# Latent attention: low halves of seven outputs and most of the paired q rotation move from VectorE to GpSimd, and the rotated q is copied four places later

## The reference, cut to what matters

```
q = (rms_norm(c_q) @ w_qup)            # 8 heads x (128 nope + 64 rope)
q_pe = rotate(q_rope)                  # t1*cos - t2*sin , t2*cos + t1*sin
s = (q_nope . k_nope + q_pe . k_pe) * scale
p = softmax(s)                         # 512 x 768 per head
o = p @ v ;  y = (o * silu(gate)) @ w_out
```

## Time and profile before

| | us |
|---|---|
| median of three timed runs | 1469.66 |
| the profiled execution's own time | 1466.62 |
| its span, first to last instruction | 1464.8 |
| PE busy | 1388.1 (95%) |
| DVE busy | 742.8 (51%) |
| ACT busy | 576.0 (39%) |
| POOL busy | 500.7 (34%) |
| attention stage, from the first scores (156.35) to the last output tile (320.04) | about 164 |

### The profile page before, as it was taken

One profiled execution on the slowest core, in us unless ns is written; L12 is line 12 of the kernel. 1 busy time (PEld: TensorE's weight loads), 2 busy tenths in 40 slices (PEclk: granted clock), 3 DMA queues, 4 the chain that ended last, 5 costly groups with the idle time before them and its releaser, 6 DMA issues.

```text
span 1464.8 us, 17904 instructions
## 1 busy us (share of the span) xinstructions
PE 1388.1 (95%) x6739; PEld 1137.9 (78%) x6739; DVE 742.8 (51%) x1003; ACT 576.0 (39%) x873; POOL 500.7 (34%) x231
## 2 busy tenths in 40 slices
PE   5899899998799999999999999989999999999998
PEld 2388677776588888877779879878888888888887
DVE  2399688841925536667543542561645435253342
ACT  4243455542433354455543343353244223132231
POOL 1134001136242295411133213214465444444441
PEclk9999999999899999999999879989999999999999
DMA  9685000117231243311223213213333333333332
GB/s 317 190 282 186 20 11 25 30 44 235 70 88 43 58 133 96 87 44 58 61 58 87 58 29 86 57 29 111 90 99 89 100 101 100 88 98 100 98 90 72
DMA packets 204500, 136.15 MB, mean 93 GB/s; under 512 B 7034, under 2 KB 185835, under 8 KB 204443
## 3 DMA queue, kind: packets, MB, share of 16 engines
q1 hardware_dynamic: 204442, 135.37, 30.8%
HBM read 130.64 MB, written 4.72 MB: 92 GB/s over the span
## 4 chain that ended last, share of the span: by engine, by line
PE 79%; DVE 11%; ACT 3%; DMA 2%; issue 2%; SPq 2%; POOL 1%; ACTq 0%; DVEq 0%; POOLq 0%
PE psum L1806 26%; PE psum L1807 24%; PE psum L1808 24%; DVE neg_max L1375 1%; DMA w_raw<-in_mla_w_in 1%; DVE pt_lo L1368 1%; PE psum L1847 1%; DVE probs L1363 1%; DMA w_raw<-in_fno_w_in 1%; POOL w_lo L596 1%; ACT probs L812 1%; PE psum L2172 1%; ACT w_hi L695 1%; PE psum L2298 0%; DVE stage L1721 0%
## 5 line engine op out<-in xcount | busy, mean ns | idle before, releaser
L596 POOL TENSOR_TENSOR w_lo<-w_raw,w_hi 128x1024 fp32r<-128x1024 f32 x180 | 437.9, 2436 | 789.8 <-ACT w_hi L695 661.8
L1806 PE MATMUL psum<-u_hi,w_hi 128*128 128x512 f32 x896 | 362.3, 404 | 14.4 <-DVE u_lo L1463 8.5
L1807 PE MATMUL psum<-u_lo,w_hi 128*128 128x512 f32 x896 | 352.7, 394 | 0.0
L1808 PE MATMUL psum<-u_hi,w_lo 128*128 128x512 f32 x896 | 352.2, 393 | 0.0
L695 ACT ACTIVATE w_hi<-w_raw 128x1024 fp32r<-128x1024 f32 x180 | 189.3, 1055 | 207.2 <-PE psum L1808 155.7
L1806 PEld LDWEIGHTS psum<-u_hi,w_hi 128*128 128x128 f32 x896 | 170.8, 191 | 60.2 <-issue 17.0
L1808 PEld LDWEIGHTS psum<-u_hi,w_lo 128*128 128x128 f32 x896 | 170.6, 190 | 36.7
L1807 PEld LDWEIGHTS psum<-u_lo,w_hi 128*128 128x128 f32 x896 | 171.0, 191 | 35.0 <-issue 1.9
L1806 PE MATMUL psum<-y_hi,w_hi 128*128 128x512 f32 x416 | 162.4, 390 | 0.0
L1807 PE MATMUL psum<-y_lo,w_hi 128*128 128x512 f32 x416 | 161.9, 389 | 0.0
L1808 PE MATMUL psum<-y_hi,w_lo 128*128 128x512 f32 x416 | 161.8, 389 | 0.0
(11 more groups left out here) (406 smaller groups left out, 2325.7 us busy)
## 6 DMA issues: line engine op xcount, KB each, us to landing
w_raw<-in_w_in SPq DMA_DIRECT2D x52, 512.0 KB, 3.7
w_raw<-in_w_up SPq DMA_DIRECT2D x32, 512.0 KB, 4.0
w_raw<-in_w_down SPq DMA_DIRECT2D x32, 512.0 KB, 3.9
ada_back<-in_w_ada SPq DMA_DIRECT2D x7, 2048.0 KB, 8.2
ada_w<-in_w_ada SPq DMA_DIRECT2D x5, 2048.0 KB, 9.3
w_raw<-in_fno_w_in SPq DMA_DIRECT2D x16, 512.0 KB, 3.8
w_raw<-in_mla_w_in SPq DMA_DIRECT2D x11, 512.0 KB, 8.8
w_raw<-in_mla_w_out SPq DMA_DIRECT2D x8, 512.0 KB, 3.9
```

The lines of the kernel that those rows point to most:

```text
L596: pool.tensor_tensor(WL[:, j, :], RAW[:, j % 2, :], f(WH[:, j, :]), ALU.subtract).then_inc(lo_done, 1)
L1806: pe.matmul(out, ah, bh, start=first, stop=False)
L1807: pe.matmul(out, ah, bl, start=False, stop=False)
L1808: return pe.matmul(out, al, bh, start=False, stop=last)
```

## The change

POOL takes over three of the four instructions of the rotation of q for heads 2, 4 and 6 (with their partners), while the shuffle stays on DVE. POOL also takes over the low halves of outputs 0 to 6; the one of the last head stays on DVE. For odd j the high and the low copy of ROPED (ACT and DVE) move from the first place of the next head's units to the place behind K_CTX. Even j keep their place. DVE's `output(j)` gets a wait for POOL's low half of output j-1, because both use the same half of `stage`. The two loads of cos and sin now count on the semaphore of the t5 loads, so that DVE's first use of the t5 tile waits for them too, and the old wait is gone.

```diff
-        s_rope = sem("rope_loaded")
+        un_swap = sem("unit_rope_swapped")
...
-        units = [(0, u) for u in first_units + (TURNED,)]
+        products = [(0, u) for u in first_units + (TURNED,)]
+        units = list(products)
         for j in range(HEADS):
-            units += [(j + 1, ROPED)] * (j < LAST) + [(j - 1, O_LAT)] * (j > 0) + [(j + 1, u) for u in (NOPED, K_LAT, K_CTX)] * (j < LAST)
+            roped, rest = [(j + 1, ROPED)] * (j < LAST), [(j - 1, O_LAT)] * (j > 0) + [(j + 1, u) for u in (NOPED, K_LAT, K_CTX)] * (j < LAST)
+            products += roped + rest
+            units += rest + roped if j % 2 else roped + rest
...
-            sp.dma_start(COS[:], d["rope_cos"]).then_inc(s_rope, 16)
-            sp.dma_start(SIN[:], d["rope_sin"]).then_inc(s_rope, 16)
+            sp.dma_start(COS[:], d["rope_cos"]).then_inc(s_t5, 16)
+            sp.dma_start(SIN[:], d["rope_sin"]).then_inc(s_t5, 16)
...
-            for h in range(HEADS):
+            def rope(j):
+
+                pool.wait_ge(un_raw, j // 2)
+                pool.wait_ge(un_lo, unit_no(j - 1, ROPED))
+                pool.tensor_tensor(QPF[:], QPR[:], COS[:], ALU.mult).then_inc(un_e, 1)
+                pool.wait_ge(un_swap, j // 2)
+                pool.tensor_tensor(SQ[:, 0, :], SQ[:, 0, :], SIN[:], ALU.mult).then_inc(un_e, 1)
+                pool.wait_ge(un_e, 3 * (j // 2))
+                pool.tensor_tensor(QPF[:], QPF[:], SQ[:, 0, :], ALU.add).then_inc(un_e, 1)
+
+            def output_lo(j):
+                pool.wait_ge(o_hi, j + 1)
+                pool.tensor_tensor(UL[:, j, :], E[:, 1, :], f(UH[:, j, :]), ALU.subtract).then_inc(o_lo, 1)
+
+            for h in range(4):
                 head_lo(h)
-            for j in range(4):
-                split_lo(MO, None, j)
+            for j in range(1, HEADS):
+                if j % 2 and j < LAST:
+                    rope(j + 1)
+                output_lo(j - 1)
+                if j < 5:
+                    head_lo(j + 3)
+                else:
+                    split_lo(MO, None, j - 5)
+            split_lo(MO, None, 3)
...
-                    act.wait_ge(un_e, j // 2 + 1)
+                    act.wait_ge(un_e, 3 * (j // 2) + 1)
...
                     if j % 2:
                         rope_raw(j + 1)
-                    unit(j + 1, ROPED)
+                    else:
+                        unit(j + 1, ROPED)
...
                     unit(j + 1, K_CTX)
+                    if j % 2:
+                        unit(j + 1, ROPED)
...
-            v.wait_ge(s_t5, 48)
+            v.wait_ge(s_t5, 80)
...
-            v.wait_ge(s_rope, 32)
...
                     v.wait_ge(un_raw, j // 2)
+                    v.wait_ge(un_e, 3 * (j // 2) - 2)
+                    v.stream_shuffle(SQ[:, 0, :], QPR[:], swap).then_inc(un_swap, 1)
                 else:
                     v.wait_ge(un_mm, unit_mm_no(0, ROPED))
-                rotate(QPF[:], QPR[:] if j else unit_out(0, ROPED), SQ[:, 0, :]).then_inc(un_e, 1)
+                    rotate(QPF[:], unit_out(0, ROPED), SQ[:, 0, :]).then_inc(un_e, 1)
...
                 v.wait_ge(tile_done, HD + j + 1)
+                if j:
+                    v.wait_ge(o_lo, j)
                 v.tensor_tensor(E[:, 1, :], out_bank(j), SG[:, j, :], ALU.mult).then_inc(o_e, 1)
...
-                if j:
-                    output_lo(j - 1)
...
-                    pe.wait_ge(un_lo, unit_no(j, K_CTX))
+                    pe.wait_ge(un_lo, max(unit_no(j, K_CTX), unit_no(j, ROPED)))
```

More of the change, by code:

```diff
@@ L391, in build @@
         first_units = (ROPED, NOPED, K_LAT, K_CTX)
-        units = [(0, u) for u in first_units + (TURNED,)]
+        products = [(0, u) for u in first_units + (TURNED,)]
+        units = list(products)
         for j in range(HEADS):
-            units += [(j + 1, ROPED)] * (j < LAST) + [(j - 1, O_LAT)] * (j > 0) + [(j + 1, u) for u in (NOPED, K_LAT, K_CTX)] * (j < LAST)
+            roped, rest = [(j + 1, ROPED)] * (j < LAST), [(j - 1, O_LAT)] * (j > 0) + [(j + 1, u) for u in (NOPED, K_LAT, K_CTX)] * (j < LAST)
+            products += roped + rest
+            units += rest + roped if j % 2 else roped + rest
+        products += [(LAST, O_LAT)]
         units += [(LAST, O_LAT)]
@@ L408, in unit_mm_no @@
         def unit_mm_no(j, u):
-            return sum(1 for x in units[:unit_no(j, u)] if not (x[1] == ROPED and x[0] % 2))
+            return sum(1 for x in products[:products.index((j, u)) + 1] if not (x[1] == ROPED and x[0] % 2))
         def out_bank(j):
```

## The result

In runs that alternate between the two kernels on one chip, the kernel before had a median of 1468.77 us (22 runs, 1466.74 to 1470.42) and the kernel after 1471.12 us (22 runs, 1469.91 to 1472.98). The ratio is 1.0017 with a 95% interval of 1.0012 to 1.0023: some 1.8 to 3.4 us slower. The ratio is within the 0.2% that was forecast, though its interval reaches 0.23%. The median is 0.5 us above the predicted 1470.6; but the forecast change was +0.9 us, and the interval leaves that out.

What follows compares the result with a forecast made beforehand. The prediction took the attention heads to be bound by a ring of waits through PE, ACT and DVE. Head terms of +0.8, +0.1, +0.1 and -0.1 made +0.9 us on 1469.66, so 1470.6 us, range 1466.3 to 1474.0.

Steps and rivals of the forecast that it cites:

- The bound: Attention heads: a ring of waits through PE, ACT and DVE, none full; an edit is worth what it moves there.
- The third rival: DVE is the true bound and its removed time comes off in full: 14.7 us, 1455.0 us; chance 0.08 with its parts.
- Joint (a): From weighing to the K_LAT product: removing DVE's rotation gains 0 in head 1 and 0.69 us in heads 3 and 5.
- Joint (b): From K_LAT to the next head's scores: the moved ROPED copy adds 0.60 us in full in heads 1, 3, 5.
- Joint (c), even heads: From scores to the next weighing, heads 2, 4, 6: without DVE's low half of output, PE gains 0.13 us each.
- Joint (c), odd heads: From scores to next weighing: POOL's low half starts some 0.3 us before DVE's scaling and holds it, +0.8 us.
- The first rival: POOL is late by 0.3 us or scaling is not blocked: no hold, -0.9 us, 1468.8 us; chance 0.27.
- The second: Rival: POOL's low half holds scaling in even heads too, with 1.74 us instructions: +4.9 us, 1474.6 us; chance 0.10.
- The sum of the heads: Head 1 +0.8, heads 2 and 3 +0.1, heads 4 and 5 +0.1, head 6 into 7 -0.1; together +0.9 us.
- some 14 us less busy in the stage: Sign in the profile after: DVE's busy time in the attention stage falls by some 14 us, the stage as long as before.
- The start: DVE's t5 copy now waits for sin, landing at 27.1 us; slack 1.3 us before PE's diagonals, so cost 0.
- the fourth rival: The change acts on the path in another way, by an unfound wait; either sign, mostly small; chance 0.10.

Runs made afterwards that it cites:

- e6_tile_waits: e1_lo_only with POOL's weight tiles of heads 2 and 4 waiting until DVE has rotated q; heads 3 and 5 took 19.22 us against 18.67, ratio to before 0.9998.
- e5_early_copy: Kernel after with odd heads' ROPED copies directly behind O_LAT and POOL's even-head weight tile behind the rotation; 1468.84 us, ratio to before 0.9993.
- e2_rope_only: Kernel after with the outputs' low halves back on DVE, rotation on POOL and moved copy kept; 1471.27 us, ratio to before 1.0018.
- e7_tile_later: e5_early_copy with POOL's even-head weight tile waiting for the ROPED low half; heads 3 and 5 took 18.38 and 18.36 us, ratio to before 0.9991.
- e3_lo_late: Kernel after with POOL's low half of each output waiting for DVE's scaling of quarter 3 of the next head; 1467.81 us, ratio to before 1.0004.
- e4_own_sem: Kernel after with cos and sin on their own semaphore again, so DVE's first t5 use doesn't wait for sin; 1471.79 us, ratio to before 1.002.
- e1_lo_only: Kernel before with only the low halves of outputs 0 to 6 moved to POOL, rotation and copy as before; 1467.51 us, ratio to before 0.999.

## Why the prediction was right and where its sum was not

The forecast time of 1470.6 us came within 0.5 us partly by luck. It started from 1469.66, the median of three runs, and over 22 runs the kernel before has 1468.77. Measured from there the forecast is 1469.7, and the change is +2.35 us where +0.9 was forecast.

**The bound.** Right. The heads are a ring of waits. DVE's windows of odd heads fell from 17.5 to 14.8 us and the heads got longer. The third rival (DVE's time comes off in full) is excluded.

**Joint (a).** Right to 0.01 us: head 3 has 6.02 us and no wait, and head 1 had nothing to gain. e6_tile_waits shows the cause, POOL's weight tile: with the tile behind the rotation, the first multiplication is at 0.69 us also with the rotation on DVE. There and in e5_early_copy the tile holds the low copy of ROPED instead.

**Joint (b), "the moved copy adds its 0.60 us in full".** Right in kind, PE waits there for `qp_hi_over_lo`. The term was mis-sized: 0.84 us in place of 0.60 in head 1 of e2_rope_only, and 5.56 - 4.74 = 0.82 us in head 3 of after. In three heads that is 0.7 us of the sum. I had taken the distance of neighbours, whose starts are closer than their lengths: the next one begins before the last has ended. This copy doesn't, on either side. It begins 0.45 us behind `kn_lo` (0.41 long), where `stage` in e7_tile_later begins after 0.33, and its successor 0.71 or 0.72 us behind it (0.69 long), where others follow after 0.60. The right price stood in the trace of before, in DVE's timeline of head 1, with the very copy that is moved:

```profile
186.30 0.69 DVE L1351 TENSOR_TENSOR qp_hi_over_lo<-qp,qp_hi_over_lo 64x512 fp32r<-64x512 f32 x1 [0.70 <-ACT qp_hi_over_lo L795]
187.02 0.69 DVE L1357 TENSOR_TENSOR o_lat_lo<-psum,o_lat_hi 128x512 fp32r<-128x512 f32 x1
```

That it has two SBUF inputs is not the reason: `u_lo` has them too and overlaps on both sides, 0.54 us behind the 0.62 us scaling and 0.60 us ahead of top. What sets the copy apart is its partitions: for an even head it reads partitions 0 to 63 and writes 64 to 127 (`QPS[lo, par, :]`, of which `lo` is the other half), while its neighbours read and write from partition 0. For an odd head it is the other way round: it reads from 64 and writes from 0. In the iteration of head 0 POOL is silent, and there DVE's timeline of before has the copy for head 1 with its successor as far behind it, 0.72 us:

```profile
168.46 0.69 DVE L1351 TENSOR_TENSOR qp_hi_over_lo<-qp,qp_hi_over_lo 64x512 fp32r<-64x512 f32 x1
169.18 0.69 DVE L1348 TENSOR_TENSOR qn_lo<-psum,qn_hi 128x512 fp32r<-128x512 f32 x1
```

So it isn't the written half alone: reading from the other half goes with the same distance. The Trainium skill (VectorE: DVE Perf Modes, Two Vector instructions with no wait between them) gives it as a model: an instruction whose output starts in another quadrant of partitions than the last output into the same memory, or one of whose inputs starts in another quadrant than what was last read from its memory, starts only when all earlier ones have finished, and so then does the next that goes back. The distances of both kinds of copy agree with it; no run here changed the partitions, so the reason is argued and only the distance is shown.

**Joint (c), even heads.** -0.13 forecast; -0.15 and -0.13 in heads 2 and 4. Head 6 gave -0.23 in place of -0.1. Together 0.1 us.

**Joint (c), odd heads, "POOL is first by some 0.3 us".** Right: first by 0.23 us, and only in odd heads. The scaling took 1.47 us, 0.85 more, where +0.8 was forecast. With the removed `u_lo` the joint is +0.29 in head 3 (8.11 - 7.82) against a forecast of +0.2. The first rival (no hold) is excluded by the rows, and e3_lo_late shows what the odd heads would have been without it: 19.07 us. The second (hold in even heads too) is excluded as well: there POOL waited.

By the Trainium skill (SBUF — State Buffer, Who interferes with whom) a `tensor_scalar` in its two-port mode and a GpSimd instruction lock each other out in full, and the order of issue decides who waits. The rows agree in who waits: 1.47 in place of 0.62 us on DVE in odd heads, 1.43 in place of 1.28 us on POOL in the even one. POOL's 0.15 us is less than the 0.30 us for which the scaling still ran, so its row doesn't show a wait in full. The same section of the Trainium skill has it that a DVE instruction with one SBUF input outside these modes isn't held, and the trace agrees there too: the shuffle under POOL takes 0.75 us (DVE's timeline of after in head 1; 0.73 alone in e6_tile_waits).

```profile
185.42 0.75 DVE L1409 STREAM_SHUFFLE squares<-qp_raw 128x512 f32<-128x512 f32 x1
```

**The sum of the heads.** Forecast: +0.8, then +0.1 for each pair, then -0.1, together +0.9. Measured: +1.09, +0.27, +0.29, -0.23, together +1.42. The difference is +0.7 (the copy), +0.2 (joint (c) of the odd heads), -0.1 (even heads) and -0.2 from the forecast's pairs, whose terms add up to 0.0 and were rounded up to +0.1: 0.6, to 0.1 us what is measured.

**DVE "some 14 us less busy in the stage".** Wrong: 8.5 us. The 14 us came from elapsed time. They held the wait for ACT's copy (3 x 0.70), which was never busy time, and left out that a held instruction counts as busy (3 x 0.85). That is 4.6 of the 5.5 us.

**The start.** Right: the wait for sin costs nothing (e4_own_sem). POOL's rotation was in time too: its last instruction in head 3, 1.29 us from 227.85, ended at 229.14, that is 5.39 us behind the start of the weighing at 223.75. It was needed 230.3 - 220.19 = 10.1 us behind it.

**What was missed.** The prediction looked at the heads and not at what follows the last, and its sign "the stage as long as before" did not come true. The last stretch is 1.55 us longer, by the clock. With the heads' 1.42 that makes +3.0 us, and the whole stage is +3.2 by the traces, beside +2.35 (1.8 to 3.4) in the times. So the forecast of +0.9 fell short by about 0.5 us in the heads and by 1.5 us in the clock. The second belongs to the fourth rival, "a wait that I did not find": the wait was in the trace of before, 2.15 us long, with full clock behind it. What in the change tips it isn't settled, nor, with two traces of each kernel, that it is the change at all. With the low halves on POOL alone it fell (e1_lo_only), but not when they wait for the scaling (e3_lo_late), nor with the weight tile behind the rotation (e6_tile_waits). That the clock costs the 1.5 us is shown in the traces: the last stretch is 22.9 to 23.0 us wherever it held, filled or not, and 24.4 to 24.5 wherever it fell. The times are too coarse for it.

## What to carry to other kernels

Time taken off an engine that isn't full is worth only what it moves in the ring of waits: walk the ring joint by joint, and price a moved instruction by the distance from start to start that its own rows show, not its neighbours'. When work goes to GpSimd, list for each of its instructions which two-input or fast-mode instruction of VectorE will stand beside it and who starts first; moving one such instruction moves the hold to the next, until it is ordered behind all that the critical chain needs (e5_early_copy, e6_tile_waits, e7_tile_later). And look at every place where TensorE waits some microseconds and then works on the path: there the clock can fall and cost 1.5 us in an edit that is meant to be neutral. Other work in the wait kept it in both kernels that tried, though their times did not show the gain.

## What the runs showed of the hardware that was not expected

- A VectorE subtraction of 64 x 512 that reads one half of the partitions and writes the other has the 0.69 us of its neighbours in the records, but no overlap with them: 0.44 to 0.45 us behind a 256-column subtraction and 0.71 to 0.72 us ahead of the next instruction, in place of 0.33 and 0.60 (before, after, e2_rope_only, e7_tile_later).
- An instruction held by GpSimd ends a fixed time behind it: 0.42 us for a scaling of 768 columns (in after), 0.54 us for a subtraction of 512 (at 280.31 before, and in e5_early_copy). The other way round, a GpSimd low half of 512 columns that starts while the scaling runs took 1.39 to 1.45 us in heads 1 to 6, in place of 1.28 to 1.30.
- Behind a wait of 2.15 to 2.17 us the TensorE clock was at 1.2 GHz for some 3 us in five kernels and at 2.4 GHz in four, and each of the three kernels traced twice repeated itself. What decides is open.
